# RWKV stage: keys' norms beside the input products, decay scans first in the chain, bonus behind, side work three turns at a time

## The chip, the cores and the metric

One core of a Trainium2 chip runs the kernel. The time is the device time of the core in microseconds (us), median of 3 runs. TensorE is PE in the profile, VectorE is DVE, ScalarE is ACT, GpSimd is POOL, SyncE (which issues all loads) is SP.

## The reference, cut to what matters

The program runs a first block (attention and feed-forward layers on 512+256 tokens), and then a second block with two layers `l` of width 1024 over 512 tokens. Each of these two layers has an attention branch, an RWKV branch, a convolution branch, a gated merge of the three, and an MLP. The change touches the RWKV branch alone:

```python
def rwkv7_branch(cols, h, v_first, ...):             # 4 heads of 64 = 256 columns
    cols = cols + (token_shift(cols) - cols) * mu    # cols = h @ w_in, 1024 columns
    r, k, v, xw, xa, xg = _split(cols, [256, 256, 256, 64, 64, 128])
    log_w = -softplus(-(w0 + tanh(xw) @ w2)) - 0.5
    decay = exp(-exp(log_w)); a = sigmoid(a0 + xa @ a2); g = sigmoid(xg) @ g2
    if layer 0: v_first = v
    else:       v = v + (v_first - v) * sigmoid(v0 + xv @ v2)   # xv = shifted h @ v1
    kk = heads(k * k_k); kk = kk / max(norm(kk), 1e-12)
    k = k * (1 + (a - 1) * k_a)
    y = wkv7_scan(r, decay, k, v, -kk, kk * a)       # the recurrence over 512 tokens
    y = group_norm(y) * ln_w + ln_b + sum(r * k * r_k) * v      # the last term: bonus
    return y * g, v_first
# merged = sigmoid(gate0) * (attention @ w_o) + sigmoid(gate1) * (y @ w_o) + ...
```

## The kernel before, in words

Activations lie with the 1024 channels on partitions (8 tiles of 128) and the 512 tokens along the free axis, all in float32. Large products split weights and activations into a high and a low part and make three matmuls of 512 columns per 128 rows: one tile of 128 output columns is 8 x 3 = 24 matmuls (`tile_pe`, L1895). For each such tile SP loads 512 KB into one of three ring slots (`stream`, L300; it waits until the slot's last user is done), ACT makes the high part (`halve_act`, L1885), POOL the low part (`halve_pool`, L1890), and PE waits for the low part. Plain float32 matmuls appear in the trace as two passes, so 4 of them are 8 instructions.

The engines run separate, in-order instruction lists. Each list is written by the same Python order: `weave` (L183) takes generators in turn, and a `yield` ends a turn. Nothing waits at a `yield` itself; only semaphores wait. Nearly all operations are recorded under a helper's line (L132 for matmuls, L142 for activations, L146, L152, L156, L164, L168 and L176 for tensor-tensor, tensor-scalar, scalar-tensor-tensor, copy, reciprocal and scan).

The RWKV stage of a layer (`rw_pe`, `rw_act`, `rw_dve`, `rw_pool`, `rw_sp`) has three parts:

1. Eight input tiles (`for n in range(8)`, L2535, L2736, L2838): 24 matmuls each, ACT copies the result into `C`, DVE makes the token-shift mix `mx` by two operations. In layer 1 there is one small tile more, `rv1` (the `xv` product). Rows of `mx`: 0 and 1 are r, 2 and 3 k (`rk`), 4 and 5 v (`rv`), 6 and 7 the inputs of the small products.
2. `chain()`: the small products `wag` (decay, a, gate; L2547), in layer 1 the v mixture (L2557, L2855), for each half n of the keys the norm `kn` by square, product with `bd64`, reciprocal, square root (L2567, L2863, L2769), the bonus `bon` (L2574, L2874), the decay scans and `Dm` (L2879), eight exponentials (L2776), eight operations that make `AR`, `a_`, `rk` (L2888), and 24 transposes with six copies (L2583, L2786).
3. `loop(0)` and `loop(1)`: four chunks of 128 tokens, 31 turns each, for two pairs of heads in turn. Each chunk builds masks, inverts a triangular matrix and carries the state `M`.

Beside parts 2 and 3 runs the side work, `merge_pe` and its partners with gate 0 (L2015 to L2067): for n = 0 to 7 a gate tile `mg` (24 matmuls) and the product `mo` of the attention output with `mla_w_o` (4 float32 matmuls). On PE one n is six turns: 6 + 6 + 6 + 6 matmuls, then `mo`, then nothing. On ACT the first turn of an n halves the gate tile of n+1 and the fifth makes the sigmoid; on POOL the first makes the low part of n+1 and the sixth adds to the merged sum; on DVE the sixth multiplies, once `mo` and the sigmoid are there. That sets the order:

```python
        weave((chain, 1), beside=(beside, 1))                      # L2504: one side turn per chain turn
        weave((loop(0), 1), (loop(1), 1), beside=(beside, 0.5))    # L2505
```

The chain has 10 rounds in layer 0 and 13 in layer 1. So 10 and 13 of the 48 side turns stand among the chain's instructions, and the rest is spread over the first 76 and 70 of the loop's rounds.

Of the kernel before, what the change touches and what calls it, by code (L numbers as in the profile page):

```python
# [7 lines left out]
ALU = mybir.AluOpType  # L8
# [4 lines left out]
TL, TC = 512, 256  # L13
# [205 lines left out]
def program(nc, T, out, ctx):  # L219
    ev = Events()  # L220
    at = ev.at
# [2311 lines left out]
    def rw_pe(pe, l):  # L2533
        rg = banks(range(8))
        for n in range(8):  # L2535
            o, before = rg.take("rw_made", "r_c", l, n)
            emptied(pe, before)
            tile_last(tile_pe(pe, l, o, 1024, ("rw", l, n), False)).then_inc(*pe.up("rw_full", l, n))
        if l:
            o, before = rg.take("rw_made", "xv")  # L2540
            emptied(pe, before)
            tile_last(tile_pe(pe, l, o[0:32, :], 256, ("rv1",), False)).then_inc(*pe.up("rw_in_full", "xv_full"))

        def chain():
            rg = banks(range(6))
            yield
            for n in range(2):  # L2547
                cs = slice(n * 128, n * 128 + 128)
                pe.wait_ge(*at("rw_made", "r_th", l))
                for j, (w, x) in enumerate(((rw2[0:64, cs], mx[0:64, 6, :]), (ra2[64:128, cs], mx[64:128, 6, :]),  # L2550
                                                (rg2[:, cs], mx[:, 7, :]))):
                    o, before = rg.take("rw_made", "wag", l, n, j)
                    emptied(pe, before)
                    pe.wait_ge(*at("ld_lora", l))
                    pe.mm(o, w, x, True, True).then_inc(*pe.up("rw_in_full", "wag_full", l, n, j))
            yield
            if l:  # L2557
                yield
                for n in range(2):
                    o, before = rg.take("rw_made", "vs", n)  # L2560
                    emptied(pe, before)
                    pe.wait_ge(*at("ld_rv2"))
                    pe.wait_ge(*at("rw_in", "xvm"))
# [3 lines left out]
            for n in range(2):  # L2567
                o, before = rg.take("rw_in", "kn", l, n)
                emptied(pe, before)
                pe.wait_ge(*at("rw_made", "kk_sq", l, n))  # L2570
                pe.wait_ge(*at("ld_bd"))
                pe.mm(o, bd64, rtm[0], True, True).then_inc(*pe.up("rw_in_full", "kn_full", l, n))
                yield
            for n in range(2):  # L2574
                o, before = rg.take("rw_in", "bon", l, n)
                emptied(pe, before)
                pe.wait_ge(*at("rw_in", "rkb", l, n))
                pe.mm(o, bd64, rtm[n], True, True).then_inc(*pe.up("rw_in_full", "bon_full", l, n))
            yield
            yield  # L2580
            yield
            pe.wait_ge(*at("rw_in", "c_ar", l))
            for j, src in enumerate((rv, a_, rk)):  # L2583
                for n in range(2):
                    o, before = rg.take("rw_made", "tr_in", l, j, n)
                    emptied(pe, before)
                    for c in range(4):
                        t = pe.tr(o[:, c * 128:c * 128 + 128], src[:, n, c * 128:c * 128 + 128], ident)
                    t.then_inc(*pe.up("rw_in_full", "tr_full", l, j, n))
            yield  # L2590
# [142 lines left out]
    def rw_act(act, l):  # L2733
        halve_act(act, 1024, "rw", l, 0)
        act.after(f"m{l}")
        for n in range(8):  # L2736
            if n < 7:
                halve_act(act, 1024, "rw", l, n + 1)
            act.wait_ge(*at("rw_full", l, n))
            act.f(C[:, n, 1:513], psum("rw_made", "r_c", l, n), ACT.Copy).then_inc(*act.up("rw_made", "r_c", l, n))  # L2740

        if l:
            halve_act(act, 256, "rv1")
            act.wait_ge(*at("rw_in_full", "xv_full"))
            act.f(xv[0:32, 1:513], psum("rw_made", "xv")[0:32, :], ACT.Copy).then_inc(*act.up("rw_made", "xv"))
        halve_act(act, 1024, "mg", l, 0, 0)

        def chain():
# [4 lines left out]
            for n in range(2):  # L2753
                for j in range(3):
# [7 lines left out]
            if l:  # L2762
                yield
                for n in range(2):
                    act.wait_ge(*at("rw_in_full", "vs_full", n))
                    act.f(kk[:, n, :], psum("rw_made", "vs", n), ACT.Sigmoid, bias=V("v0", n)).then_inc(*act.up("rw_made", "vs", n))
                    yield
            yield
            for n in range(2):  # L2769
                act.wait_ge(*at("rw_in", "kk", l, n))  # L2770
                act.f(rtm[0], kk[:, n, :], ACT.Square).then_inc(*act.up("rw_made", "kk_sq", l, n))
                act.wait_ge(*at("rw_in", "kn_r", l, n))
                act.f(rtm[0], rtm[0], ACT.Sqrt).then_inc(*act.up("rw_made", "kn_rs", l, n))
                yield
# [9 lines left out]
            yield  # L2784
            yield
# [49 lines left out]
    def rw_dve(dve, l):  # L2835
        dve.after(f"m{l}")
        dve.memset(C[:, :, 0:1], 0.0).then_inc(*dve.up("rw_in", "r_c0"))
        for n in range(8):  # L2838
            dve.wait_ge(*at("rw_made", "r_c", l, n))
            dve.tt(dif[n % 2], C[:, n, 0:TL], C[:, n, 1:513], ALU.subtract).then_inc(*dve.up("rw_in", "r_mx"))  # L2840
            dve.stt(mx[:, n, :], dif[n % 2], V(f"mu{l}", n), C[:, n, 1:513], ALU.mult, ALU.add).then_inc(*dve.up("rw_in", "r_mx", l, n))

        def chain():
            yield
            yield
            dve.wait_ge(*at("rw_made", "wag", l, 1, 2))
            if l == 0:
                dve.cp(vfirst[:, :].rearrange("p (k t) -> p k t", k=2), rv).then_inc(*dve.up("rw_in", "vf"))
            else:
                dve.memset(xv[0:32, 0:1], 0.0).then_inc(*dve.up("rw_in", "xvm_"))  # L2850
                dve.wait_ge(*at("rw_made", "xv"))
                dve.tt(rtm[0][0:32, :], xv[0:32, 0:TL], xv[0:32, 1:513], ALU.subtract).then_inc(*dve.up("rw_in", "xvm_"))
                dve.stt(rtm[1][0:32, :], rtm[0][0:32, :], V("v_mu")[0:32, :], xv[0:32, 1:513], ALU.mult, ALU.add).then_inc(*dve.up("rw_in", "xvm"))
                yield
                for n in range(2):  # L2855
                    dve.tt(rtm[0], vfirst[:, n * TL:n * TL + TL], rv[:, n, :], ALU.subtract).then_inc(*dve.up("rw_in", "vf"))
                    dve.wait_ge(*at("rw_made", "vs", n))
                    dve.tt(rtm[0], rtm[0], kk[:, n, :], ALU.mult).then_inc(*dve.up("rw_in", "vf"))
                    dve.tt(rv[:, n, :], rv[:, n, :], rtm[0], ALU.add).then_inc(*dve.up("rw_in", "vf"))
                    yield  # L2860
            yield
            dve.ts(omk, V(f"k_a{l}", 0, 2), -1.0, 1.0, ALU.mult, ALU.add).then_inc(*dve.up("rw_in", "omk"))
            for n in range(2):  # L2863
                dve.ts(kk[:, n, :], rk[:, n, :], V(f"k_k{l}", n), None, ALU.mult, None).then_inc(*dve.up("rw_in", "kk", l, n))
                dve.wait_ge(*at("rw_in_full", "kn_full", l, n))
                dve.ts(rtm[0], psum("rw_in", "kn", l, n), 1e-24, None, ALU.max, None).then_inc(*dve.up("rw_in", "kn", l, n))
                dve.recip(rtm[0], rtm[0]).then_inc(*dve.up("rw_in", "kn_r", l, n))
                dve.wait_ge(*at("rw_made", "kn_rs", l, n))
                dve.tt(kk[:, n, :], kk[:, n, :], rtm[0], ALU.mult).then_inc(*dve.up("rw_in", "ka_"))
                dve.ts(rtm[1], a_[:, n, :], V(f"k_a{l}", n), omk[:, n:n + 1], ALU.mult, ALU.add).then_inc(*dve.up("rw_in", "ka_"))  # L2870
                dve.tt(rk[:, n, :], rk[:, n, :], rtm[1], ALU.mult).then_inc(*dve.up("rw_in", "ka_"))
                dve.tt(a_[:, n, :], a_[:, n, :], kk[:, n, :], ALU.mult).then_inc(*dve.up("rw_in", "ka_"))
                yield
            for n in range(2):  # L2874
                dve.stt(rtm[n], rr[:, n, :], V(f"r_k{l}", n), rk[:, n, :], ALU.mult, ALU.mult).then_inc(*dve.up("rw_in", "rkb", l, n))
                dve.wait_ge(*at("rw_in_full", "bon_full", l, n))
                dve.tt(bon[:, n, :], psum("rw_in", "bon", l, n), rv[:, n, :], ALU.mult).then_inc(*dve.up("rw_in", "bon", l, n))
            dve.wait_ge(*at("ld_cmf", l))
            for n in range(2):  # L2879
                dve.scan(cc[:, n, :], cmf, s_[:, n, :]).then_inc(*dve.up("rw_in", "r_cc"))  # L2880
            yield
            for n in range(2):
                c4 = cc[:, n, :].rearrange("p (c t) -> p c t", c=4)
                d4 = Dm[:, n, :].rearrange("p (c t) -> p c t", c=4)
                dve.stt(d4, bc(c4[:, :, 127], 2, 128), -0.5, c4, ALU.mult, ALU.add).then_inc(*dve.up("rw_in", "Dm", l, n))
            yield
# [6 lines left out]
            yield  # L2893
# [67 lines left out]
    def rw_pool(pool, l):  # L2961
# [414 lines left out]
```

## Time and profile before

| | us |
|---|---|
| median of 3 runs | 4376.97 (4371.32 to 4385.71) |
| the profiled execution | 4379.5 |
| its span in the trace | 4377.7 |
| PE busy | 3900.5 (89%) |
| DVE busy | 1839.0 (42%) |
| ACT busy | 1316.9 (30%) |
| POOL busy | 430.5 (10%) |

The chain of work that ended last is PE for 75% of the span, DVE for 13% and ACT for 6%. A busy time is a sum over instructions; a granted clock of 1.00 is TensorE's full 2.4 GHz, 0.50 is 1.2 GHz. In the rows below, a number in brackets is the idle time of the engine just ahead of the instruction, and behind the arrow stands what ended it.

### The profile page before, as it was taken

To read this page: it belongs to the slowest core of one execution; us is meant where nothing else is said; L and a number is where in the kernel's file an instruction comes from. 1 tells how busy PE (TensorE), PEld (TensorE's weight loads), DVE (VectorE), ACT (ScalarE), POOL (GpSimd) and SP (SyncE) were. 2 spreads that over 40 slices of the span, in tenths; PEclk is the share of its full clock that TensorE was granted. 3 is DMA by queue.
4 is the path that set the end of the run, shared out by engine and by line. 5 is a ranking of instruction groups with operands and counts; after the bars stand their busy time and mean duration, and the time that the engine had idled before them with its cause. 6 is when DMAs were issued, how large, how long until landed. Compare 5 with 4: busy or idle time off the path is not lost.

```text
span 4377.7 us, 52573 instructions
## 1 busy us (share of the span) xinstructions
PE 3900.5 (89%) x21392; PEld 3033.8 (69%) x21392; DVE 1839.0 (42%) x2826; ACT 1316.9 (30%) x1960; POOL 430.5 (10%) x277
## 2 busy tenths in 40 slices
PE   7788888999997988999888879899998887989999
PEld 3555547788886777788766657678876664767887
DVE  2544443533343334444443354544334335454433
ACT  3332322322133233322334321232233432123222
POOL 0211110000002110000101211000011121100000
PEclk9878779999998999999989989999999998999999
DMA  4112252121211222223211201123322121112332
GB/s 157 62 41 82 78 193 87 49 68 58 68 50 53 86 87 65 86 96 103 67 53 35 76 23 45 45 89 96 96 74 57 32 76 28 41 40 93 96 96 68
DMA packets 320320, 317.03 MB, mean 72 GB/s; under 512 B 8720, under 2 KB 286128, under 8 KB 319952
## 3 DMA queue, kind: packets, MB, share of 16 engines
q1 hardware_dynamic: 320080, 313.67, 22.6%
q8 instruction: 169, 2.77, 0.3%
q14 instruction: 71, 0.58, 0.0%
HBM read 311.55 MB, written 2.10 MB: 72 GB/s over the span
## 4 chain that ended last, share of the span: by engine, by line
PE 75%; DVE 13%; ACT 6%; DMA 3%; issue 2%; POOL 2%; SPq 0%; DVEq 0%; ACTq 0%; POOLq 0%
PE PS L132 74%; DVE scr L146 5%; ACT scr L142 4%; DMA ring<-in_ada_w 1%; DVE PS L160 1%; DVE scr L156 1%; DMA scr<-in_na_bias 1%; DVE NBt L156 1%; PE PS L135 1%; DVE scr L168 1%; POOL na_w L146 1%; DVE scr L164 1%; ACT L142 0%; DVE scr L152 0%; DVE scr L176 0%
## 5 line engine op out<-in xcount | busy, mean ns | idle before, releaser
L132 PE MATMUL PS<-scr 128*32 128x32 f32 (+7 forms) x6692 | 659.2, 283 | 134.4 <-DVE scr L146 77.6
L132 PEld LDWEIGHTS PS<-scr 128*128 128x128 f32 (+4 forms) x6692 | 537.9, 170 | 282.8 <-issue 128.0
L132 PE MATMUL PS<-ffn_h,ffn_w 128*128 128x512 f32 (+1 forms) x3168 | 615.6, 357 | 8.4 <-DVE ffn_h L156 5.7
L132 PEld LDWEIGHTS PS<-ffn_h,ffn_w 128*128 128x128 f32 x3168 | 524.4, 189 | 100.8 <-issue 9.7
L142 ACT ACTIVATE scr<-PS 128x256 f32<-128x256 f32 (+4 forms) x489 | 231.5, 473 | 1015.4 <-PE PS L132 943.2
L146 DVE TENSOR_TENSOR scr<-scr 128x512 f32<-128x512 f32 (+3 forms) x419 | 284.5, 679 | 280.7 <-ACT scr L142 244.8
L132 PE MATMUL PS<-h_h,ring_r 128*128 128x512 f32 (+1 forms) x976 | 363.7, 434 | 41.0 <-POOL ring_r L146 31.2
L132 PE MATMUL PS<-mlp_h,mlp_w 128*128 128x512 f32 x1536 | 364.3, 399 | 5.5 <-DVE mlp_h L146 5.0
L132 PE MATMUL PS<-mlp_g,mlp_w 128*128 128x512 f32 x1536 | 359.7, 396 | 0.0
L132 PEld LDWEIGHTS PS<-mlp_h,mlp_w 128*128 128x128 f32 x1536 | 291.3, 190 | 79.8 <-issue 9.4
L132 PEld LDWEIGHTS PS<-mlp_g,mlp_w 128*128 128x128 f32 x1536 | 288.7, 188 | 69.7
L164 DVE COPY scr<-PS 128x256 f32<-128x256 f32 (+7 forms) x300 | 143.8, 479 | 400.5 <-PE PS L132 392.0
L132 PE MATMUL PS<-ffn_g,ffn_w 128*128 128x512 f32 (+1 forms) x1584 | 305.4, 355 | 0.0
L132 PEld LDWEIGHTS PS<-ffn_g,ffn_w 128*128 128x128 f32 x1584 | 261.1, 188 | 43.6
L142 ACT ACTIVATE scr<-scr 128x256 f32<-128x256 f32 (+8 forms) x340 | 172.0, 506 | 347.6 <-DVE scr L146 150.9
L132 PEld LDWEIGHTS PS<-h_h,ring_r 128*128 128x128 f32 (+1 forms) x976 | 196.0, 201 | 96.1 <-issue 36.9
L146 POOL TENSOR_TENSOR NBt<-NBt 128x256 f32<-128x256 f32 (+1 forms) x70 | 79.0, 1129 | 1852.7 <-ACT NBt L142 1847.8
L146 DVE TENSOR_TENSOR mlp_w<-ring,mlp_w 128x2048 fp32r<-128x2048 f32 x80 | 183.4, 2293 | 120.0 <-ACT mlp_w L142 120.0
L146 DVE TENSOR_TENSOR scr<-PS,scr 128x256 f32<-128x256 f32 (+4 forms) x256 | 132.0, 516 | 237.3 <-PE PS L132 200.4
L146 DVE TENSOR_TENSOR ffn_w<-ring,ffn_w 128x2048 fp32r<-128x2048 f32 (+1 forms) x76 | 170.0, 2237 | 136.0 <-ACT ffn_w L142 135.8
L142 ACT ACTIVATE mlp_w<-ring 128x2048 fp32r<-128x2048 f32 x80 | 153.9, 1924 | 221.5 <-PE PS L132 216.5
L146 POOL TENSOR_TENSOR scr<-scr 128x256 f32<-128x256 f32 (+2 forms) x120 | 126.4, 1053 | 842.9 <-ACT scr L142 442.9
(150 smaller groups left out, 4730.5 us busy)
## 6 DMA issues: line engine op xcount, KB each, us to landing
ring<-in_ada_w SPq DMA_DIRECT2D x48, 1024.0 KB, 6.0
ring<-in_ffn_w_in SPq DMA_DIRECT2D x44, 1024.0 KB, 5.1
ring<-in_w_up SPq DMA_DIRECT2D x32, 1024.0 KB, 5.4
ring<-in_w_down SPq DMA_DIRECT2D x32, 1024.0 KB, 5.1
ring<-in_w_in SPq DMA_DIRECT2D x60, 512.0 KB, 3.9
ring<-in_ffn_w_out SPq DMA_DIRECT2D x16, 1024.0 KB, 5.0
scr<-in_na_bias SPq DMA_DIRECT2D x32, 512.0 KB, 5.5
ring<-in_na_w_qkv SPq DMA_DIRECT2D x24, 512.0 KB, 4.0
```

What stands on the lines that cost most here:

```text
L132: return self.eng.matmul(o, lhsT=l, rhs=r, start=start, stop=stop) if self.eng else Nothing()
L135: return self.eng.transpose(o, i, idn) if self.eng else Nothing()
L142: return self.eng.activation(o, i, func, bias=bias, scale=scale, accum_out=total) if self.eng else Nothing()
L146: return self.eng.tensor_tensor(o, a, b, op) if self.eng else Nothing()
L156: return self.eng.scalar_tensor_tensor(out=o, in0=a, scalar=s, in1=b, op0=op0, op1=op1) if self.eng else Nothing()
L160: return self.eng.tensor_tensor_reduce(o, a, b, 1.0, first, op0, op1, total) if self.eng else Nothing()
L164: return self.eng.tensor_copy(o, i) if self.eng else Nothing()
L168: return self.eng.reciprocal(o, i) if self.eng else Nothing()
```

## The change

Side work gets three turns per turn of the chain. The keys' norms move out of the chain into the input tiles: DVE multiplies by `k_k` after tile 3, ACT squares after tile 4, PE multiplies with `bd64` behind tile 5, DVE clamps and inverts in the same turn, ACT takes the roots after tile 6. In the chain the small products go by kind (decay for both halves first), the scans follow the decay at once, the v transposes come ahead of the exponentials' users, and the bonus comes last. ACT halves `rv1` (layer 1) or the first gate tile (layer 0) one step earlier, ahead of the copy of tile 7. The chain has 6 yields, so 7 rounds, in both layers, and 21 side turns.

```diff
     def rw_turns(chain, loop, beside):
-        weave((chain, 1), beside=(beside, 1))
+        weave((chain, 1), beside=(beside, 3))
...
+            if n == 5:
+                for i in range(2):
...
+                    pe.wait_ge(*at("rw_made", "kk_sq", l, i))
+                    pe.mm(o, bd64, rtm[i], True, True).then_inc(*pe.up("rw_in_full", "kn_full", l, i))
     # rw_pe, chain
-            for n in range(2):
-                for j, (w, x) in enumerate(...):
+            for j in range(3):
+                for n in range(2):
...
             yield
             if l:
-                yield
                 for n in range(2):
...
-                    yield
-            yield
-            for n in range(2): ...                    # kn: take, wait kk_sq, matmul, yield
-            for n in range(2): ...                    # bon: take, wait rkb, matmul
-            yield
-            yield
-            yield
-            pe.wait_ge(*at("rw_in", "c_ar", l))
+            yield
             for j, src in enumerate((rv, a_, rk)):
+                if j == 0:
+                    pe.wait_ge(*at("rw_in", "rv", l))
+                else:
+                    pe.wait_ge(*at("rw_in", "c_ar", l))
...
+                if j == 0:
+                    yield
+                    yield
+            for n in range(2): ...                    # bon
             yield
     # rw_act, input tiles
-            if n < 7:
-                halve_act(act, 1024, "rw", l, n + 1)
+            halve_act(act, *((1024, "rw", l, n + 1) if n < 7 else (256, "rv1") if l else (1024, "mg", l, 0, 0)))
             act.wait_ge(*at("rw_full", l, n))
             act.f(C[:, n, 1:513], psum("rw_made", "r_c", l, n), ACT.Copy)...
+            for i in range(2):
+                if n == 4:
+                    act.wait_ge(*at("rw_in", "kk", l, i))
+                    act.f(rtm[i], kk[:, i, :], ACT.Square)...
+                elif n == 6:
+                    act.wait_ge(*at("rw_in", "kn_r", l, i))
+                    act.f(rtm[i], rtm[i], ACT.Sqrt)...
         if l:
-            halve_act(act, 256, "rv1")
+            halve_act(act, 1024, "mg", l, 0, 0)
...
-        halve_act(act, 1024, "mg", l, 0, 0)
     # rw_act, chain: wag by kind; [vs]; then
-            for n in range(2): ...                    # Square, Sqrt, yield
             for n in range(2): ...                    # eight exponentials
-            yield
-            yield
             for j, dst in enumerate((vt, bt, ktk)):
...
+                if j == 0:
+                    yield
+                    yield
     # rw_dve, input tiles, after the two operations of tile n
+            for i in range(2):
+                if n == 3:
+                    dve.ts(kk[:, i, :], rk[:, i, :], V(f"k_k{l}", i), None, ALU.mult, None)...
+                elif n == 5:
+                    dve.wait_ge(*at("rw_in_full", "kn_full", l, i))
+                    dve.ts(rtm[i], psum("rw_in", "kn", l, i), 1e-24, None, ALU.max, None)...
+                    dve.recip(rtm[i], rtm[i])...
+        for n in range(2):
+            dve.wait_ge(*at("rw_made", "kn_rs", l, n))
+            dve.tt(kk[:, n, :], kk[:, n, :], rtm[n], ALU.mult)...
     # rw_dve, chain after the change
+            yield
+            ...        # layer 0: copy of v; layer 1: the xv mix
+            yield
+            dve.wait_ge(*at("ld_cmf", l))
+            for n in range(2):
+                dve.wait_ge(*at("rw_made", "wag", l, n, 0))
+                dve.scan(cc[:, n, :], cmf, s_[:, n, :])...
                 dve.stt(d4, bc(c4[:, :, 127], 2, 128), -0.5, c4, ALU.mult, ALU.add)...      # Dm
+            yield
+            if l: ...  # the v mix, three operations per half, wait vs
+            for n in range(2):
+                dve.wait_ge(*at("rw_made", "wag", l, n, 1))
+                dve.ts(dif[n], a_[:, n, :], V(f"k_a{l}", n), omk[:, n:n + 1], ALU.mult, ALU.add)...
+                dve.tt(rk[:, n, :], rk[:, n, :], dif[n], ALU.mult)...
+                dve.tt(a_[:, n, :], a_[:, n, :], kk[:, n, :], ALU.mult)...
+            for n in range(2):
+                dve.stt(rtm[n], rr[:, n, :], V(f"r_k{l}", n), rk[:, n, :], ALU.mult, ALU.mult)...
+            yield
+            yield
             dve.wait_ge(*at("rw_made", "ec", l, 1))
...
+            for n in range(2):
+                dve.wait_ge(*at("rw_in_full", "bon_full", l, n))
+                dve.tt(bon[:, n, :], psum("rw_in", "bon", l, n), rv[:, n, :], ALU.mult)...
             yield
     # rw_pool
-            for _ in range(9 + 3 * (l > 0)):
+            for _ in range(6):
                 yield
```

## Rows read from the trace of the kernel before

**Rows 1.** Stretches: busy time (and instructions) of each engine, granted clock, DMA share.
```profile
core 0: us, PE busy (x) PEld busy (x) DVE busy (x) ACT busy (x) POOL busy (x), PEclk, DMA share, GB/s
2513.60:2578.90 65.30, 34.88 (x100) 20.88 (x100) 32.53 (x35) 24.16 (x35) 9.04 (x4) 0.74 0.07 20
2578.90:2606.50 27.60, 22.60 (x121) 18.16 (x121) 16.24 (x25) 3.96 (x8) 3.61 (x2) 0.88 0.10 29
2606.50:2659.00 52.50, 49.95 (x305) 38.76 (x304) 25.37 (x49) 10.68 (x22) 10.36 (x6) 1.00 0.17 46
...
2720.80:2761.60 40.80, 33.42 (x238) 29.39 (x237) 22.45 (x48) 5.71 (x16) 1.27 (x1) 0.87 0.03 9
2761.60:2780.80 19.20, 18.58 (x135) 15.45 (x133) 8.12 (x21) 3.13 (x9) 0.00 (x0) 1.00 0.01 2
...
3595.30:3677.00 81.70, 50.71 (x142) 27.43 (x142) 38.52 (x44) 25.93 (x40) 10.30 (x6) 0.73 0.10 29
...
3597.20:3603.10 5.90, 5.72 (x24) 2.52 (x24) 0.49 (x1) 0.05 (x1) 0.00 (x0) 1.00 0.03 10
3607.30:3613.80 6.50, 6.45 (x14) 2.84 (x14) 0.00 (x0) 2.04 (x3) 2.37 (x1) 0.54 0.00 0
```

**Rows 2.** Timeline of PE, layer 0: start, us, engine, operation, count, idle before.
```profile
2518.06 0.77 PE L132 MATMUL PS<-h_h,ring_r 128*128 128x512 f32 x1 [4.49 <-POOL ring_r L146]
2528.74 1.10 PE L132 MATMUL PS<-scr,KC 128*128 128x512 f32 x2 [0.71 <-ACT scr L142]
2538.61 2.07 PE L132 MATMUL PS<-scr,KC 128*128 128x512 f32 x2 [7.38 <-ACT scr L142]
2549.07 2.07 PE L132 MATMUL PS<-scr,KC 128*128 128x512 f32 x2 [4.46 <-DVE scr L156]
2571.20 5.00 PE L135 MATMUL PS<-KC,scr 128*128 128x128 f32 x24 [11.84 <-DVE scr L146]
2578.91 2.96 PE L132 MATMUL PS<-scr 64*128 64x256 f32 x16
2581.80 3.70 PE L132 MATMUL PS<-scr,ring 128*128 128x512 f32 x8
```

**Rows 3.** Timeline of PE, layer 1.
```profile
3597.29 0.40 PE L132 MATMUL PS<-h_h,ring_r 128*32 128x512 f32 x1 [2.09 <-POOL ring_r L146]
3607.35 0.77 PE L132 MATMUL PS<-h_h,ring_r 128*128 128x512 f32 x1 [4.34 <-POOL ring_r L146]
```

**Rows 4.** Timeline of ACT, layer 0.
```profile
2508.05 0.60 ACT L142 ACTIVATE scr<-PS 128x512 f32<-128x512 f32 x1 [3.79 <-PE PS L132]
2513.60 0.60 ACT L142 ACTIVATE scr<-PS 128x512 f32<-128x512 f32 x1 [4.95 <-PE PS L132]
...
2547.51 1.28 ACT L142 ACT_TABLE_LOAD   x1
2559.69 3.64 ACT L142 ACTIVATE scr<-scr 128x512 f32<-128x512 f32 x8 [10.90 <-DVE scr L156]
2589.42 1.06 ACT L142 ACTIVATE ring_r<-ring 128x1024 fp32r<-128x1024 f32 x1 [9.81 <-DMA ring<-in_w_in]
```

**Rows 5.** Timeline of DVE, both layers.
```profile
2530.60 3.35 DVE L168 RECIPROCAL scr<-scr 128x512 f32<-128x512 f32 x1
2555.62 2.48 DVE L176 TENSOR_TENSOR_SCAN scr<-scr 128x512 f32<-128x512 f32 x2
...
3636.59 3.50 DVE L146 TENSOR_TENSOR scr<-scr 128x512 f32<-128x512 f32 x2
...
3649.53 1.42 DVE L146 TENSOR_TENSOR scr<-scr 128x512 f32<-128x512 f32 x2
...
3665.26 0.69 DVE L156 SCALAR_TENSOR_TENSOR scr<-scr 128x512 f32<-128x512 f32 x1 [2.98 <-ACT scr L142]
...
3668.89 2.15 DVE L146 TENSOR_TENSOR scr<-scr 128x512 f32<-128x512 f32 x3
```

**Rows 6.** Timeline of POOL: a low part in layer 1, a sum in layer 0.
```profile
3636.48 2.34 POOL L146 TENSOR_TENSOR ring_r<-ring,ring_r 128x1024 fp32r<-128x1024 f32 x1 [8.19 <-ACT ring_r L142]
...
2588.62 1.27 POOL L146 TENSOR_TENSOR scr<-scr 128x512 f32<-128x512 f32 x1 [21.65 <-DVE scr L146]
```

More of the change, by code:

```diff
@@ L2538, in rw_pe @@
             tile_last(tile_pe(pe, l, o, 1024, ("rw", l, n), False)).then_inc(*pe.up("rw_full", l, n))
+            if n == 5:
+                for i in range(2):
+                    o, before = rg.take("rw_in", "kn", l, i)
+                    emptied(pe, before)
+                    pe.wait_ge(*at("rw_made", "kk_sq", l, i))
+                    pe.wait_ge(*at("ld_bd"))
+                    pe.mm(o, bd64, rtm[i], True, True).then_inc(*pe.up("rw_in_full", "kn_full", l, i))
         if l:
@@ L2546, in chain @@
             yield
-            for n in range(2):
[L2548 to L2551, printed above, removed]
+            pe.wait_ge(*at("rw_made", "r_th", l))
+            pe.wait_ge(*at("ld_lora", l))
+            for j in range(3):
+                for n in range(2):
+                    cs = slice(n * 128, n * 128 + 128)
+                    w, x = ((rw2[0:64, cs], mx[0:64, 6, :]), (ra2[64:128, cs], mx[64:128, 6, :]), (rg2[:, cs], mx[:, 7, :]))[j]
                     o, before = rg.take("rw_made", "wag", l, n, j)
                     emptied(pe, before)
-                    pe.wait_ge(*at("ld_lora", l))
                     pe.mm(o, w, x, True, True).then_inc(*pe.up("rw_in_full", "wag_full", l, n, j))
@@ L2563, in chain @@
                     pe.wait_ge(*at("rw_in", "xvm"))
-                    pe.mm(o, rv2[0:32, n * 128:n * 128 + 128], rtm[1][0:32, :], True, True).then_inc(*pe.up("rw_in_full", "vs_full", n))
-                    yield
+                    pe.mm(o, rv2[0:32, n * 128:n * 128 + 128], dif[1][0:32, :], True, True).then_inc(*pe.up("rw_in_full", "vs_full", n))
             yield
[L2567 to L2572, printed above, removed]
-                yield
[L2574 to L2578, printed above, removed]
-            yield
-            yield
-            yield
-            pe.wait_ge(*at("rw_in", "c_ar", l))
             for j, src in enumerate((rv, a_, rk)):
+                if j == 0:
+                    pe.wait_ge(*at("rw_in", "rv", l))
+                else:
+                    pe.wait_ge(*at("rw_in", "c_ar", l))
                 for n in range(2):
@@ L2589, in chain @@
                     t.then_inc(*pe.up("rw_in_full", "tr_full", l, j, n))
+                if j == 0:
+                    yield
+                    yield
+            for n in range(2):
+                o, before = rg.take("rw_in", "bon", l, n)
+                emptied(pe, before)
+                pe.wait_ge(*at("rw_in", "rkb", l, n))
+                pe.mm(o, bd64, rtm[n], True, True).then_inc(*pe.up("rw_in_full", "bon_full", l, n))
             yield
@@ L2752, in chain @@
             yield
-            for n in range(2):
-                for j in range(3):
+            for j in range(3):
+                for n in range(2):
                     act.wait_ge(*at("rw_in_full", "wag_full", l, n, j))
@@ L2762, in chain @@
             if l:
-                yield
                 for n in range(2):
                     act.wait_ge(*at("rw_in_full", "vs_full", n))
-                    act.f(kk[:, n, :], psum("rw_made", "vs", n), ACT.Sigmoid, bias=V("v0", n)).then_inc(*act.up("rw_made", "vs", n))
-                    yield
[L2768 to L2774, printed above, removed]
+                    act.f(rtm[n], psum("rw_made", "vs", n), ACT.Sigmoid, bias=V("v0", n)).then_inc(*act.up("rw_made", "vs", n))
             yield
@@ L2851, in chain @@
                 dve.wait_ge(*at("rw_made", "xv"))
[L2852 to L2860, printed above, removed]
@@ L2861, in chain @@
-            yield
[L2862 to L2877, printed above, removed]
+                dve.tt(dif[0][0:32, :], xv[0:32, 0:TL], xv[0:32, 1:513], ALU.subtract).then_inc(*dve.up("rw_in", "xvm_"))
+                dve.stt(dif[1][0:32, :], dif[0][0:32, :], V("v_mu")[0:32, :], xv[0:32, 1:513], ALU.mult, ALU.add).then_inc(*dve.up("rw_in", "xvm"))
@@ L2878, in chain @@
+            yield
             dve.wait_ge(*at("ld_cmf", l))
-            for n in range(2):
-                dve.scan(cc[:, n, :], cmf, s_[:, n, :]).then_inc(*dve.up("rw_in", "r_cc"))
-            yield
             for n in range(2):
@@ L2892, in chain @@
                 dve.tt(rk[:, n, :], rk[:, n, :], EN[:, n, :], ALU.mult).then_inc(*(dve.up("rw_in", "c_ar", l) if n else dve.up("rw_in", "c_ar")))
-            yield
+            for n in range(2):
+                dve.wait_ge(*at("rw_in_full", "bon_full", l, n))
+                dve.tt(bon[:, n, :], psum("rw_in", "bon", l, n), rv[:, n, :], ALU.mult).then_inc(*dve.up("rw_in", "bon", l, n))
             yield
```

24 lines of the change are left out of this document (19 added, 5 removed).

## The prediction

> **What bounds the kernel now.** The page first: PE is busy for 89% of the span and makes 75% of the chain that ended last, so time is to be had only where PE stands idle or runs at the low clock, or where work beside it is stretched. Next the stretches of the RWKV stage [rows 1]. The chain takes 65.3 us in layer 0 and 81.7 us in layer 1, with PE busy for 34.88 and 50.71 us of it at a granted clock of 0.74 and 0.73. The loop that follows is of two kinds: with side work a piece of 52.5 us has PE busy for 49.95; without any, one chunk from one X0 transpose to the next takes 40.8 us with PE busy for 33.42. So in the chain PE has room, and in the loop the side work costs time. Third the timelines [rows 2 to 4] for which wait ends last. In layer 0 PE waits 4.49 us for the low part of the first gate tile, 7.38 us behind the first key norm, 4.46 us at the bonus, 11.84 us ahead of the transposes: 30.5 us with the small ones (65.3 less 34.88). Two reciprocals of 3.35 us [rows 5] lie on this path, one behind the other.
>
> **The change part by part.** I lay out the new order by hand, with durations from rows. One matmul of a split tile is 5.55 / 24 = 0.231 us (two copies of successive tiles, 2508.05 and 2513.60 [rows 4]), so three side turns (18 matmuls) are 4.2, the fourth 1.4 and `mo` 3.7 us [rows 2].
>
> *Input tiles.* PE gets the two norm products, 4 passes, 2 x 1.1 = 2.1 us at the full clock (2528.74 [rows 2]); I use 1.9 since a pass starts before the last one ends. They push tiles 6 and 7 back by 1.9 us in each layer. DVE gets 8.2 us behind tile 5 (two of 0.69 and two of 3.35): from 2504.7 to 2512.9 in old time, and tile 7's result comes at 2515.5, so nothing waits. ACT's roots end near 2513.6, ahead of tile 7's copy. If the reciprocals were slowed by POOL by 2.4 us each, 2 us would show; bounds 0 and 4 us a layer.
>
> *First gate tile.* It is halved before tile 7's copy: ACT done 2514.7, POOL 2.5 us, PE starts at 2517.3 instead of 2518.06, with an idle time of about 2 instead of 4.49. After an idle 2.09 PE kept clock 1.00, after 4.34 it ran at 0.54 [rows 1, 3], so I give this part the full clock. In layer 1 `rv1` and the gate tile are both ready in time: the idle 2.09 and 4.34 us go, and PE starts the gate tile at 3602.6 instead of 3607.35.
>
> *The chain, layer 0.* PE: 18 matmuls to 2521.5, `wag` 4.0 to 2525.5, 1.4 and 3.7 to 2530.5, 18 matmuls of the second tile to 2534.7, 8 transposes (24 took 5.00 [rows 2]) to 2536.3, 5.1 to 2541.4, 18 matmuls of the third tile to 2545.6. DVE's scans now stand behind its `mo` multiplication, so they start at 2531.3, not at 2524; scans 2.48 and `Dm` 1.4 to 2535.3; the key and bonus operations 5.5 to 2540.8. What is new on ACT: in front of the exponentials stands the halving of gate tile 2, and its load waits for the ring slot that `mo` 0 frees at 2530.5. The nearest row is the idle time of 9.81 us that ended with such a load [rows 4]; it landed 3.9 us after the PE work that freed its slot. So ACT has 2534.4, 1.06 for halving, 1.28 for a table load, 3.64 for the exponentials (2540.3), 1.3 for two copies, another 1.28, 0.6 for the sigmoid: 2543.5. DVE's second `mo` multiplication waits for that sigmoid, and the eight operations `AR` are queued behind it: 2544.4 instead of 2540.8. This wait is the price of the three turns here. `AR` takes 5.8 us undisturbed (3665.26 to 3668.89 + 2.15 [rows 5]).
>
> Now POOL's low part of tile 3 and a sum fall into `AR`. The row: two tensor-tensor operations took 3.50 us beside POOL's 2.34 us and 1.42 without it [rows 5, 6], so 2.1 us more, and for a sum of 1.27 at most 1.3 more. The Trainium skill (SBUF — State Buffer, on the shared port pair) says that a DVE operation with two SBUF inputs and a GpSimd operation lock each other out for the whole instruction; by that, too, 3.4 us would be added here; the trace agrees. `AR` then ends between 2550.2 and 2553.6; I take 2552.5. PE: 16 transposes 3.3, bonus 3.7 (half the passes at the low clock, as 2.07 at 2549.07 [rows 2]), side turns 1.4 + 3.7 + 4.2, and 0.2 of gaps: the loop starts at 2569 instead of 2578.91, 10 us earlier, with 21 side turns done instead of 10. Bounds 6 and 13.
>
> *The chain, layer 1.* The same from 3602.6: `mo` 0 done 3615.8, two `vs` products 2.1, scans done at 3620.6, then the v mix (six operations, 4.3, plus 2.1 beside POOL) to 3627, for which the first transposes wait 4.9 us; transposes, rest of tile 1 and `mo` 1 at a partly low clock to 3634.5; `AR` from 3635.3 with 8.7 us to 3644; 16 transposes, bonus and 9.3 us of side turns: the loop starts at about 3659 instead of 3677.03. That is 18 us, bounds 13 and 22. The gain is larger because the three extra rounds of the v part with their waits are gone and the start is 4.8 us earlier.
>
> One table load sits between the halving and the exponentials. The row shows 1.28 us and the next instruction with no further gap [rows 4]. The Trainium skill (ScalarE: Activation LUTs, What ACT_TABLE_LOAD costs) counts a drain of about 1.38 us more per switch; by it four loads on the path of the two layers would cost 5.5 us more and the time would be 4333.5. The row decides: nothing is added.
>
> *The loop.* Without side work it is 27.6 + 3 x 40.8 + 19.2 = 169.2 us [rows 1] (the first piece still holds two side tiles' turns, so this is an upper value). Before, layer 0 takes 201.9 with 38 side turns, layer 1 199.5 with 35, so one side turn costs about 1 us, against 1.5 us of PE work (9.25 us in six turns). Now 27 turns are left; they end in round 54, between the X0 transposes of chunks 1 and 2 (rounds 45 and 76). So the loop is 27.5 to the first X0, 55 to the second, 41 + 4.5 turns = 46, then 40.8 and 19.2: 188.5. That is 13 and 11 us less. By the price per turn it is 11 and 8. I take 12 and 9. The bounds: nothing, if the room in the chunks is then merely left empty, and 17 and 12 us, if every us of PE work taken out counted.
>
> *POOL, SP.* POOL's empty turns cost nothing. SP's order is unchanged; loads of tiles 2 and 3 start when `mo` 0 and `mo` 1 are done, earlier than before, in a stretch with a DMA share of 0.07 [rows 1].
>
> The sum: -10 -12 in layer 0, -18 -9 in layer 1, -49 us. From the profiled execution's 4379.5 that is 4330.5; this execution was 2.5 us above the median of the runs, so the forecast is 4328 us, 1.1% faster.
>
> **The rivals.**
> (a) The loop gives nothing back: its length is set by DVE and ACT latencies and the side work filled holes. For it: PE is idle 7.4 of 40.8 us in a chunk without side work. Against it: the chunks with side work take 52.5 and more. Then only 28 us are gained: 4349.
> (b) The chain overlaps better than I laid out (full clock throughout, no wait at `mo` 1, bounds 13, 17, 22, 12 of above): 4377 - 64 = 4313.
> (c) Slower: the three side turns stand in PE's in-order list between a producer and its user, so they lengthen the chain instead of filling holes. The place is the 17.0 us of extra side work in layer 0 (`mo` 1, tile 2, `mo` 2, three turns of tile 3) and 12.0 in layer 1. If all chain waits stay as long as they are and the loop isn't shorter, the time is 4377 + 29 = 4406. It decides from the point at which a side block is longer than the wait it stands in: blocks are 4.2 and 5.1 us, the waits of PE were 7.38 and 11.84 [rows 2], which speaks against it; and the two norm waits leave the chain altogether.
> (d) The norms are moved but don't hide: the reciprocals and roots hold up tiles 6 and 7 by 8.2 us a layer, for a slot or a bank. Against it: DVE idles 4 us of each 5.55 there, and ACT as much. The gain falls to 49 - 16 = 33: 4344.
>
> **How the numbers follow.** The forecast with its own range (4318 to 4338) 0.52; (a) 0.17, (b) 0.13, (d) 0.12, (c) 0.06. The range reaches from (b) to (a): 4312 to 4352. Within 0.3% (13 us, about what a measurement of this kernel can tell from no change) needs the gain to fall below 13 us, which only something between (a) and (c) would do: 0.04. Faster 0.91, slower 0.05.
>
> **What would show it.** The loop's first matmuls of 64 rows (2578.91 now) come about 10 us earlier in layer 0 and, seen from the end of the input tiles, 18 us in layer 1; the last side `mo` ends near the X0 transpose of chunk 1; two chunks of 40.8 us without side work instead of one. DVE's reciprocals lie inside the input tiles, which last 1.9 us longer. PE's longest wait in the chain is about 7 us ahead of the 16 transposes, behind `AR`. ACT waits for the load of gate tile 2 ahead of the exponentials. I am wrong if the loop keeps 200 us, or if PE's waits in the chain sum to more than 20 us a layer.

## The result and the profile after

The median is 4318.18 us (4314.40 to 4325.29, 4 runs) against 4377.42; the ratio of the runs is 0.9864, 95% interval 0.9849 to 0.9878. That is 59 us less, where 49 were forecast (4328). The median lies at the lower edge of the forecast's own range (4318 to 4338), nearer to rival (b)'s 4313 than to 4328. The profiled execution took 4325.29 us, 54.2 less than that of before.

Stretches of the kernel after (columns as in [rows 1]): the chain of layer 0 behind tile 7, four pieces of its loop (the start, the chunk with most side turns, the one in which they end, one without any), the chain of layer 1. A chunk is counted from its X0 transpose, the first 128x128 transpose of it, to the next chunk's.

```profile
2516.30:2572.00 55.70, 46.95 (x155) 31.05 (x155) 29.11 (x31) 22.64 (x34) 12.69 (x7) 0.85 0.19 52
2572.00:2596.10 24.10, 21.64 (x122) 17.33 (x122) 15.29 (x25) 4.77 (x9) 6.01 (x3) 0.93 0.12 33
2596.10:2648.70 52.60, 50.22 (x305) 38.80 (x304) 24.64 (x49) 9.62 (x21) 8.80 (x5) 1.00 0.18 54
2648.70:2697.20 48.50, 40.63 (x264) 34.07 (x263) 22.45 (x48) 6.30 (x17) 1.41 (x2) 0.89 0.10 30
2697.20:2738.00 40.80, 33.42 (x238) 29.38 (x237) 22.18 (x48) 5.71 (x16) 0.00 (x0) 0.87 0.00 1
3574.60:3637.90 63.30, 51.03 (x181) 32.30 (x179) 35.01 (x39) 25.61 (x37) 14.27 (x7) 0.89 0.18 50
```

In the chains PE is busy for 84% and 81% of the time, where it was 53% and 62% [rows 1]. The chunk without side work is the same as before, 40.8 us. There is still one such chunk in each loop; the prediction's last part announced two, although its own sum has only one (27.5, 55, 46, 40.8, 19.2). Here the last side turns reach into the chunk before it, which takes 48.5 us.

PE's timeline in layer 0 (columns as in [rows 2]): the norm products behind tile 5, the first gate tile, every wait of over 2 us up to the loop, and the loop's start.

```profile
2502.82 1.88 PE L132 MATMUL PS<-scr,KC 128*128 128x512 f32 x4
2517.89 0.66 PE L132 MATMUL PS<-h_h,ring_r 128*128 128x512 f32 x1 [2.10 <-POOL ring_r L146]
...
2546.66 0.79 PE L132 MATMUL PS<-h_h,ring_r 128*128 128x512 f32 x1 [4.27 <-ACT scr L142]
...
2556.47 3.67 PE L135 MATMUL PS<-KC,scr 128*128 128x128 f32 x16 [2.88 <-DVE scr L146]
...
2571.96 2.96 PE L132 MATMUL PS<-scr 64*128 64x256 f32 x16
```

The waits of 7.38 and 4.46 us at the norms and the bonus are gone, and 11.84 us ahead of the transposes became 2.88. The forecast's 2 us ahead of the gate tile are there, and the norm products take 1.88 us, where 1.9 was used. All waits of PE in this stretch sum to 8.8 us (55.70 less 46.95), in layer 1 to 12.3, so the sign of being wrong (over 20) did not show. The longest was forecast as some 7 us ahead of the 16 transposes; it is another one, which was not foreseen: PE waits 4.27 us for gate tile 2, since its bank is freed by ACT's sigmoid, and ACT stood still before:

```profile
2537.16 1.06 ACT L142 ACTIVATE ring_r<-ring 128x1024 fp32r<-128x1024 f32 x1 [7.03 <-DMA ring<-in_w_in]
2538.30 1.28 ACT L142 ACT_TABLE_LOAD   x1
2539.60 3.64 ACT L142 ACTIVATE scr<-scr 128x512 f32<-128x512 f32 x8
2543.33 1.29 ACT L142 ACTIVATE scr<-PS 128x512 f32<-128x512 f32 x2
2544.71 1.28 ACT L142 ACT_TABLE_LOAD   x1
2546.01 0.60 ACT L142 ACTIVATE scr<-PS 128x512 f32<-128x512 f32 x1
```

This is ACT's order as forecast (load of tile 2, halving, exponentials, copies, sigmoid), some 3 us later than forecast. DVE, in the same stretch, waits 11.10 us at its first side multiplication with the scans queued behind it, and `AR` (2547.50 to 2556.42) takes 8.9 us beside POOL's 3.9 us of work. The same eight operations take 5.8 us in a_arfirst (below), where POOL is idle beside them:

```profile
2532.57 0.69 DVE L146 TENSOR_TENSOR scr<-PS,scr 128x512 f32<-128x512 f32 x1 [11.10 <-PE PS L132]
...
2546.69 0.69 DVE L146 TENSOR_TENSOR scr<-PS,scr 128x512 f32<-128x512 f32 x1 [0.57 <-ACT scr L142]
2547.50 1.79 DVE L156 SCALAR_TENSOR_TENSOR scr<-scr 128x512 f32<-128x512 f32 x1
2549.32 4.19 DVE L146 TENSOR_TENSOR scr<-scr 128x512 f32<-128x512 f32 x3
2553.54 0.69 DVE L156 SCALAR_TENSOR_TENSOR scr<-scr 128x512 f32<-128x512 f32 x1
2554.27 2.15 DVE L146 TENSOR_TENSOR scr<-scr 128x512 f32<-128x512 f32 x3
```

POOL's work also fell on operations for which the forecast added nothing. The first scan took 2.32 us and the first tensor-scalar operation of the key part 2.40; in a_rate1, with POOL idle beside them, they took 1.72 and 0.55.

### The profile page after: what moved, and what is told of

Same layout as the page of the kernel before. It is cut to its first block, busy times and chain, and to the rows that moved or that the text cites. A ratio compares the mean times of both kernels' runs of the same rounds, so it can differ in the third digit from the quotient of the medians.

```text
span 4323.5 us, 52579 instructions
## 1 busy us (share of the span) xinstructions
PE 3888.6 (90%) x21392; PEld 3030.3 (70%) x21392; DVE 1850.3 (43%) x2826; ACT 1320.7 (31%) x1963; POOL 432.1 (10%) x277
## 4 chain that ended last, share of the span: by engine, by line
PE 74%; DVE 12%; ACT 6%; DMA 3%; POOL 2%; issue 2%; SPq 0%; DVEq 0%; ACTq 0%; POOLq 0%
PE PS L132 74%; DVE scr L146 5%; ACT scr L142 4%; DMA ring<-in_ada_w 1%; DVE PS L160 1%; DMA scr<-in_na_bias 1%; DVE scr L156 1%; DVE NBt L156 1%; PE PS L135 1%; POOL na_w L146 1%; ACT L142 1%; DVE scr L164 1%; DVE scr L168 1%; DVE NBt L146 0%; POOL NBt L146 0%
## 5 line engine op out<-in xcount | busy, mean ns | idle before, releaser
L146 POOL TENSOR_TENSOR ring_r<-ring,ring_r 128x1024 fp32r<-128x1024 f32 (+1 forms) x61 | 146.9, 2408 | 585.3 <-ACT ring_r L142 584.6
```

Of the source, the lines that this page charges most:

```text
L146: return self.eng.tensor_tensor(o, a, b, op) if self.eng else Nothing()
```

## The experiments

Two lengths per layer describe every run, each read from PE's timeline of its own profiled execution. "Chain" goes from the end of tile 5 (where the norm products start, or 0.2 us ahead of ACT's copy of tile 5 where they are elsewhere) to the first matmul of 64 rows; "loop" from there to the product with `bd64` behind the loop. "Turns" are the side turns left for the loop. Ratios are to the kernel before on the same chip (its medians on the others were 4377.5, 4380.9 and 4380.6).

| kernel | chain 0, 1 | turns | loop 0, 1 | sum | median us | ratio (95%) |
|---|---|---|---|---|---|---|
| before | 76.6, 93.1 | 38, 35 | 201.9, 199.5 | 571.1 | 4377.4 | 1 |
| after | 69.1, 77.0 | 27 | 185.3, 184.4 | 515.8 | 4318.2 | 0.9864 (0.9849-0.9878) |
| b_norms | 60.1, 79.4 | 38, 35 | 204.5, 199.0 | 543.0 | 4350.2 | 0.9938 (0.9922-0.9954) |
| b_rate2 | 90.2, 113.7 | 28, 22 | 191.9, 182.0 | 577.8 | 4385.2 | 1.0015 (1.0004-1.0027) |
| a_rate1 | 45.3, 56.2 | 41 | 210.0, 209.6 | 521.1 | 4330.8 | 0.9900 (0.9880-0.9921) |
| a_bare | 67.4, 77.2 | 0 | 157 bare | | 4350.6 | 0.9939 (0.9923-0.9955) |
| a_spread | 67.4, 77.0 | 27 | 193.8, 193.8 | 532.0 | 4343.6 | 0.9915 (0.9899-0.9930) |
| a_dense | 69.1, 77.2 | 27 | 188.8, 188.0 | 523.1 | 4328.4 | 0.9884 (0.9868-0.9899) |
| a_arfirst | 63.2, 69.2 | 27 | 184.5, 185.2 | 502.1 | 4314.5 | 0.9851 (0.9834-0.9867) |
| a_scans | 63.7, 70.4 | 27 | 184.2, 184.3 | 502.6 | 4314.7 | 0.9856 (0.9840-0.9872) |
| a_early | 57.8, 66.3 | 27 | 186.5, 184.7 | 495.3 | 4305.7 | 0.9833 (0.9817-0.9849) |
| e_dense | 57.7, 66.3 | 27 | 189.6, 188.6 | 502.2 | 4308.7 | 0.9835 (0.9820-0.9851) |
| e_rate2 | 60.0, 71.0 | 34 | 194.4, 196.7 | 522.1 | 4331.5 | 0.9898 (0.9873-0.9923) |
| e_rate4 | 72.4, 81.8 | 20 | 178.9, 176.8 | 509.9 | 4320.9 | 0.9861 (0.9844-0.9877) |

The lengths repeat within 3 us: the same chain code took 67.4 to 69.1 us in layer 0 in four kernels, the loop with the same 27 turns at the same rate 184.2 to 186.5 in four, and the unchanged loop of b_norms 204.5 for 201.9. The rest of the profiled execution, outside the sum, varies from 3802 to 3811 us, which is why the sums tell more than the times.

**b_norms.** The kernel before with the norms' edit alone.

```diff
 # rw_pe, input tiles (rw_act and rw_dve as in the change); the chain keeps its yields
+            if n == 5:
+                for i in range(2):
...
+                    pe.mm(o, bd64, rtm[i], True, True).then_inc(*pe.up("rw_in_full", "kn_full", l, i))
 # rw_pe, chain
             for n in range(2):
-                pe.mm(o, bd64, rtm[0], True, True).then_inc(*pe.up("rw_in_full", "kn_full", l, n))
                 yield
```

> The kernel before with one part of the change alone: the keys' norms are made beside the input tiles, the rest of the chain keeps its order and its one side turn per chain turn. Theory N (the norms' waits were the largest part of the chain): DVE's stretch from the first norm to the bonus, about 21.7 us in layer 0, shrinks to 4, PE's input tiles get 1.9 us longer, the loop keeps its side turns and its 200 us: 12 to 15 us a layer, 4348 to 4353. Rival S (the side turns bring it all, since PE's list was the long one in the chain): less than 5 us a layer, over 4367.

Measured 4350.2, as N has it and not S. The chains shrink by 16.5 and 13.7 us; the loops stay within 3 us. In each layer 10.7 us of that is idle time of PE; the rest is the same work at a granted clock of 0.83, where it was 0.78 and 0.76. This is half of the gain of the sums (28.1 of 55.3 us).

**b_rate2.** Only the rate of the side turns, in the kernel before.

```diff
-        weave((chain, 1), beside=(beside, 1))
+        weave((chain, 1), beside=(beside, 2))
```

> The kernel before with only the number of side turns in the chain changed, two per chain turn: 20 in layer 0 and 26 in layer 1, about as many as the change has, with all norm waits left in the chain. If side work fills the chain's holes and a turn costs 1 us in the loop (the prediction's price): the chain grows by some 5 us, the loop shrinks by 10 and 13, together -13, 4364. If a turn taken from the loop is worth its whole PE work or more (1.5 to 1.9 us, as the two traces suggest): the loop shrinks by 16 and 20, 4351. If the turns lengthen the chain by their own length (rival c): about 4377 or above.

Measured 4385.2, 0.15% slower, in the third case (4377 or above): rival (c)'s mechanism, without the rest of the change. The loops gave 10.0 and 17.5 us, the chains grew by 13.6 and 20.6. The window from the same tile on, compared with the first of [rows 1], shows where:

```profile
2513.60:2592.50 78.90, 49.47 (x153) 30.27 (x153) 36.92 (x37) 26.42 (x38) 13.98 (x7) 0.83 0.12 35
```

PE is busy 14.6 us longer (49.47 against 34.88), and its idle time is 29.4 against 30.4: the side turns hardly filled the holes.

**a_rate1.** The changed kernel with one side turn per chain turn.

```diff
-        weave((chain, 1), beside=(beside, 3))
+        weave((chain, 1), beside=(beside, 1))
```

> The changed kernel with one side turn per chain turn, so 7 turns in the chain and 41 in the loop; norms and order as changed. At 1 us a turn in the loop: loops of 199, the chain some 8 us shorter than with 21 turns, 4330. At 1.5 to 1.9 us a turn: loops of 206 to 212, 4346. If the side turns had been worth nothing: 4318 less what the chain gets shorter, about 4302.

Measured 4330.8 in the median, the first number, but by another way: the loops are 210, as the dear price has it, and the chain is 24 and 21 us shorter, not 8. So norms and order alone bring 50.0 of the 55.3 us, the order some 22 of them (571.1, 543.0, 521.1; it also moves 3 and 6 turns to the loop, since the chain has fewer rounds). Going from one turn to three is 5.3 us by the sums; by the medians it is 12.6. This kernel's profiled execution (4323.2) was the fastest of its four, that of the changed kernel (4325.3) the slowest of its four, and the intervals of the two ratios just miss each other. So the step pays, by an amount between the two that isn't settled.

**a_bare.** No side turns in the loop, all 27 behind it.

```diff
-        weave((loop(0), 1), (loop(1), 1), beside=(beside, 0.5))
+        weave((loop(0), 1), (loop(1), 1))
```

> The changed kernel with no side turns in the loop at all: the 27 turns left of each layer come behind the loop. It shows the loop's bare length. If the price of a turn is a constant 1 us, the loop is 185 - 27 = 158 us; if the first turns are cheap and only the later ones cost their whole PE work (holes get filled first), the loop is about 166 (four chunks of 40.8 and the ends). The side work behind it takes 27 x 1.54 = 42 us a layer or more, so the whole is 4347 by the first and 4366 or more by the second.

Measured 4350.6, near the first number (4347, a constant price). Its chunks, from one X0 transpose to the next:

```profile
2595.00:2630.00 35.00, 27.63 (x222) 25.28 (x220) 21.88 (x47) 5.72 (x16) 0.00 (x0) 0.90 0.00 1
2630.00:2670.30 40.30, 32.93 (x238) 28.88 (x237) 22.20 (x49) 5.72 (x16) 0.00 (x0) 0.92 0.01 1
2670.30:2710.90 40.60, 33.23 (x238) 29.18 (x237) 22.18 (x49) 5.72 (x16) 0.00 (x0) 0.87 0.00 0
```

With 21.7 us ahead of the first and 19.2 behind the last the bare loop is 157 us, so the first 27 turns cost 28 us, 1.05 each. My 166 had taken the first chunk for a full one; it has no state and takes 35. The prediction's 169.2 did the same, and kept 27.6 us for the piece ahead of it, which takes 21.7 bare.

**a_spread and a_dense.** The 27 turns at another density.

```diff
-        weave((loop(0), 1), (loop(1), 1), beside=(beside, 0.5))
+        weave((loop(0), 1), (loop(1), 1), beside=(beside, 0.25))   # a_spread; a_dense: 1
```

> The changed kernel, with the 27 side turns left for the loop dealt at half the rate (a turn every four rounds, to round 108 of 125) and not at 0.5 (to round 54). The run without side turns in the loop shows a bare loop of 157 us against 185 with them. Theory H (side turns fill the holes of a chunk until the chunk is full; PE is idle for about 7 us of each bare chunk of 40.8): spread out they fill all four chunks' holes, loops of 170 to 175, 4290 to 4300. Theory P (a side turn stands in PE's in-order list and delays a chain of small dependent steps by nearly its own length wherever it stands): no change, 4312 to 4325.

> The changed kernel with the 27 side turns of the loop dealt at rate 1 instead of 0.5 (to round 27 of 125, all within chunk 0). Dealt at 0.25 the loops took 194 us, at 0.5 they took 185, all behind the loop 157 + 42 = 199. Theory D (the denser the cheaper, since a full PE keeps its clock at 1.00 while a chunk with a quarter of a turn per round had 0.90 and still 7.6 us idle): loops of 178 to 182, 4306 to 4312. Theory F (chunk 0 is full at 0.5 already, what comes on top costs its whole PE work, while chunk 1 loses turns that cost 1.8 us each): loops of 183 to 187, 4314 to 4322.

Neither theory of either pair holds. Spread out the loops get 9 us longer (4343.6), which neither H nor P had. Made dense they get 3.5 us longer (4328.4): D had the wrong sign, F the right kind, but loops and median lie beyond its upper end. The second chunk of a_spread, and the dense stretch of a_dense with the chunk behind it:

```profile
2642.70:2694.20 51.50, 43.90 (x276) 35.89 (x274) 24.39 (x48) 7.37 (x18) 3.63 (x2) 0.90 0.06 16
```

```profile
2566.30:2599.70 33.40, 32.37 (x159) 23.56 (x159) 15.90 (x26) 6.38 (x11) 9.69 (x5) 1.00 0.17 48
2599.70:2654.70 55.00, 47.92 (x294) 38.73 (x293) 23.44 (x48) 8.57 (x20) 6.19 (x4) 0.94 0.20 63
```

About eight turns make a chunk of 40.3 us one of 51.5 (1.4 us a turn), and PE stays idle for 7.6 us, as in the bare chunk. In the changed kernel 15.5 turns make the first chunk, 35.0 us bare, one of 52.6 (1.1 us a turn), with 2.4 us idle at clock 1.00 (above). My reading is that a hole is closed only once side work lies all around it; no run tests that by itself, and in the dense kernel 13 turns leave 7.1 us idle.

**a_arfirst, a_scans, a_early.** Three chain orders; side work and amounts stay.

```diff
 # a_arfirst, DVE chain
-            yield
-            yield
             dve.wait_ge(*at("rw_made", "ec", l, 1))
...
+            yield
+            yield
             for n in range(2):
                 dve.wait_ge(*at("rw_in_full", "bon_full", l, n))
 # a_scans, DVE: the yield between the copy of v (xv mix) and the scans goes behind Dm
 # a_scans, ACT: the yield ahead of the exponentials goes behind them
 # a_early: all of it
```

> The changed kernel, with DVE's eight operations AR moved ahead of its second side multiplication (mo 1), which waits for PE's mo 1 and ACT's sigmoid. The trace of the changed kernel has AR start 1.4 us (layer 0) and 3.5 us (layer 1) after the operation ahead of that multiplication. If AR sets the transposes' time: 5 us less, 4313. If PE's own list is what sets them: no change, 4318.

> The changed kernel, with DVE's scans and Dm moved ahead of its first side multiplication (mo 0; DVE idles 11.1 us ahead of it in the changed kernel) and ACT's exponentials ahead of the halving of gate tile 2 (7 us of waiting for its load in layer 0). By the hand-made order: PE's transposes come 3.7 us earlier in layer 0 (AR still waits for mo 1) and about 6 in layer 1, where the v transposes wait for DVE: 4308. If PE's list is full by itself: within 3 us of 4318.

> Both edits together: scans ahead of mo 0's multiplication, exponentials ahead of tile 2's halving, AR ahead of mo 1's multiplication. By the hand-made order PE reaches the 16 transposes 9.5 us earlier in layer 0 and about 12 in layer 1, with hardly any idle time ahead of them: 4297. If the two waits hide each other's gain only in part, the sum of the two single edits: 4303.

a_arfirst shortens the chains by 5.9 and 7.8 us, more than the 1.4 and 3.5 forecast: `AR` also escapes POOL's work (5.8 us for 8.9). a_scans gives 5.4 and 6.6, against 3.7 and 6 forecast, and the two together 11.3 and 10.7. That is 22.0, less than their sum of 25.7 and close to the 21.5 laid out by hand; the median is 9 us above the 4297 expected all the same, 3.5 of it from the kernel before on this chip. The times alone don't tell a_arfirst and a_scans from the changed kernel (the intervals overlap); the stretches do. The chain of layer 0 of a_early:

```profile
2502.40:2560.20 57.80, 54.27 (x208) 36.71 (x206) 37.00 (x39) 29.06 (x41) 16.31 (x9) 0.97 0.23 64
```

PE is busy for 94% of it: what is left is PE's own list. With 4305.7 us it is, together with e_dense, the fastest kernel here, 0.9833 against 0.9864; the intervals touch, the stretches show 20.5 us.

**e_dense, e_rate2, e_rate4.** a_early with loop rate 1, and with two or four turns in the chain.

> The kernel with scans, exponentials and AR early (4306 with rate 0.5 in the loop), and rate 1 in the loop. By D 4294 to 4300, by F 4302 to 4310. Sum of two edits that don't touch: the difference to 4306 is that of the kernel above to 4318.

> The kernel with scans, exponentials and AR early, with two side turns per chain turn instead of three (14 in the chain, 34 in the loop). In the changed kernel the step from one turn to three cost the chain 24 and 21 us and gave the loop 25 and 25 back. If that still holds, about even: 4304 to 4310. If the shorter chain has no holes left for the third turn: faster, below 4300. If the loop's full chunks are the dearer place: 4314 and more.

> The same with four side turns per chain turn (28 in the chain, 20 in the loop). Loop by the price of the first turns (1.05 us each): 7 us a layer shorter; the chain longer by the turns' PE work, 10.8 us a layer, less what idle time is left in it (about 5). Between 4303 and 4313; if DVE or ACT waits move behind side work: 4320.

e_dense (4308.7) is within F: the loops cost 3.1 and 3.9 us more, as in a_dense. e_rate2 (4331.5) is the dear case: the chain does not get shorter (60.0 and 71.0 against 57.8 and 66.3), since a hole opens ahead of the 16 transposes, 9.71 us where a_early has 1.43, and the loops are 8 and 12 us longer:

```profile
2548.59 3.67 PE L135 MATMUL PS<-KC,scr 128*128 128x128 f32 x16 [9.71 <-DVE scr L146]
```

e_rate4 gives 7.6 and 7.9 us in the loop and takes 14.6 and 15.5 in the chain, and at 4320.9 it is the second case, not the 4303 to 4313. Three is the best of the rates tried with this order; one was not tried with it.

## Why the prediction came out right, point by point

| step | forecast | measured |
|---|---|---|
| norm products in the input tiles | +1.9 a layer, nothing else late | ACT's copy of tile 7 came 1.7 later, by the copies of tiles 5 and 7 |
| loop's start, layer 0 | -10 | -7.5 |
| loop's start, layer 1 | -18 | -16.1 |
| loop, layer 0 | -12 | -16.6 |
| loop, layer 1 | -9 | -15.1 |
| sum | -49 | -55.3 |

The total is right and the mechanism is right in part. b_norms shows that the norms' waits were on the path; a_rate1 that the new order was worth 22 us more. Rival (d) is out: DVE's reciprocals (2505.96 to 2513.50) were done ahead of tile 7's result. Rival (a) is out: the loops got shorter by 15 us and more. But the forecast's chains were 4.4 us too good and its loops 10.7 us too poor, in layer 1 beyond its own bound of 12. Part of the closeness of the sum is luck.

The mis-sized term is the loop. I took about 1 us a turn and let pieces with an unchanged number of turns keep their length. The average price holds: 20 turns cost 21 us (e_rate4), 27 turns 28. But in the kernel before 38 turns cost 45 and 35 cost 42, and 41 turns 53 in a_rate1. The loop read piece by piece, from its start by the X0 transposes (in brackets the side turns in the piece):

| piece | a_bare | after, layer 0 | before, layer 0 | before, layer 1 | a_rate1, layer 0 |
|---|---|---|---|---|---|
| to the first X0 | 21.7 (0) | 24.1 (7) | 27.6 (7) | 26.9 (7) | 28.6 (7) |
| first chunk | 34.9 (0) | 52.6 (15.5) | 52.5 (15.5) | 58.6 (15.5) | 59.1 (15.5) |
| second | 40.3 (0) | 48.5 (4.5) | 61.7 (15.5) | 54.1 (12.5) | 57.1 (15.5) |
| third | 40.6 (0) | 40.8 (0) | 40.8 (0) | 40.8 (0) | 45.8 (3) |
| behind the last | 19.2 (0) | 19.2 (0) | 19.2 (0) | 19.2 (0) | 19.2 (0) |

```profile
2659.00:2720.80 61.80, 55.81 (x322) 43.64 (x321) 23.95 (x50) 8.57 (x20) 5.55 (x4) 0.94 0.17 50
3703.90:3762.40 58.50, 52.98 (x311) 41.81 (x310) 24.45 (x48) 10.33 (x22) 9.63 (x5) 0.94 0.12 32
```

```profile
2570.80:2629.95 59.15, 53.63 (x311) 42.24 (x310) 24.45 (x48) 10.19 (x22) 9.66 (x5) 0.94 0.11 32
```

(The first fence is the kernel before: second chunk of layer 0, first chunk of layer 1; the second is the first chunk of a_rate1.) Of the 16.6 us that layer 0's loop lost, 13.3 lie in the second chunk, which lost 11 turns (1.2 us each), and 3.5 in the piece ahead of the first X0, which kept its seven. Of layer 1's 15.1 us only 5.8 lie in the chunk that lost turns; 9.3 lie in the two pieces that kept theirs. So the gain beyond the forecast isn't the price of the turns taken out, and no single price fits: the first seven turns cost 2.4 us, the last 4.5 cost 8.2.

What goes with the length of the pieces that kept their number is which turns they are. A gate tile and its `mo` are six turns, and the first chunk takes 58.4 to 59.1 us in the four loops of rate 0.5 that start one turn into such a group (layer 1 of before and b_norms, a_rate1), with 17.0 to 17.5 us of ACT's waits for loads of gate tiles. It takes 53.7 to 56.8 in those that start two turns in (b_rate2, e_rate2), 52.6 to 53.9 three turns in (after and the orders built on it), 52.5 and 53.8 four turns in (layer 0 of before and b_norms); with three ACT waits 9 us there, with four 4.2 to 4.5. The number left does not order them: 38 turns left give 52.5, 22 give 53.7. It also fits b_rate2, whose loop with 28 turns took 191.9. No run moved this place alone, so the cause stays open, and the comparisons of two, three and four turns in the chain carry it along.

The second error lies in the picture of the chain, where two mistakes worked against each other. I let the side turns fill PE's waits there, some 13 us of them in a layer (a_rate1 was expected to have a chain only 8 us shorter for 14 turns fewer). They filled none; the norms' move and the order had taken those waits out by themselves. PE's idle time in layer 0's chain (from the end of tile 5) was 30.5 us before, 19.8 in b_norms, 8.4 in a_rate1 and 9.3 after; in layer 1 it was 31.1, 20.4, 11.6 and 12.3. From one turn to three the chain got 24 and 21 us longer for 21.2 us of PE work (60 matmuls and two `mo`), and in the old chain 13.6 and 20.6 us. Rival (c) had this right, and its other half, an unchanged loop, wrong. Its place in the prediction was weighed by comparing blocks of 4.2 and 5.1 us with waits of 7.38 and 11.84, waits that were gone by then. So the title's third part, side work three turns at a time, was nearly a swap of chain time for loop time: 5 us of 55 by the stretches, 13 of 59 by the medians. The chain was 2.5 and 1.9 us slower than forecast; in layer 0 the first gate tile alone took 1.7 us more, at a lower clock, and POOL's work beside the first scan and the key part 2.5 us more on DVE.

## What to carry to other kernels

Here filler work in in-order lists cost about its own length in a chain of dependent steps, and left PE's idle time as it was; measure its price at both places (move a few turns) before taking it for free, and read the loop piece by piece, since its pieces changed length with the same number of turns. What did pay was to move a chain of small dependent steps out, beside PE's long input products, and to put each engine's chain steps ahead of the filler step that waits: one or two `yield`s moved gave 5 to 8 us a layer by the stretches.

## What the runs showed of the hardware that was not expected

Tanh and Sigmoid at the head of the chain cost no table load before the change. Behind the Sqrt of the norms they cost two, one ahead of each, 1.28 us apiece; b_norms, which moves only the norms, shows the same two. From tile 6's copy to the loop ACT has 4 and 3 such loads before and 5 and 5 after:

```profile
2516.51 1.28 ACT L142 ACT_TABLE_LOAD   x1
2519.12 0.63 ACT L142 ACTIVATE scr<-scr 64x512 f32<-64x512 f32 x1 [1.33 <-DVE scr L156]
2519.77 1.28 ACT L142 ACT_TABLE_LOAD   x1
2521.06 0.63 ACT L142 ACTIVATE scr<-scr 128x512 f32<-128x512 f32 x1
```

An idle time of 2.10 us was followed here by a gate tile at a granted clock of 0.71 (18 matmuls in 5.9 us instead of 4.2), where one of 2.09 us in the kernel before left it at 1.00 [rows 1, 3]. So an idle time near 2 us doesn't say by itself which clock comes after it:

```profile
2517.90:2523.80 5.90, 5.90 (x19) 4.40 (x19) 3.40 (x6) 3.61 (x4) 0.88 (x1) 0.71 0.21 64
```
